# Sample recurrences with one eight-column product per state, and woven dense products taken column by column

## The chip, the core and the metric

The kernel runs on one core of one Trainium2 chip. The metric is the device time of one execution in microseconds; the profile beside it is of one execution. The engines are named as the profile names them: PE (matmul) and PEld (its weight load), DVE (vector), ACT (scalar), POOL and SP (here mostly issuers of transfers).

## The reference

One decoder layer for a prompt of 256 rows and 8 sample sequences of 4 rows, all with a model width of 2048 and with shared weights. Cut to what matters here:

```
h = x + 1/2 * SwiGLU_1(RMSNorm(x))
u = RMSNorm(h); P = u @ w_in
y_A = GatedDeltaNet(...)   # S_t = exp(g_t)(I - beta_t k_t k_t^T) S_{t-1} + beta_t k_t v_t^T ; o_t = S_t^T q_t
y_B = GLA(...)             # S_t = diag(exp(gk_t)) S_{t-1} + k_t v_t^T ;               o_t = S_t^T q_t
y_C = RWKV-7(...)          # S_t = S_{t-1} diag(w_t) + (S_{t-1} a_t) b_t^T + v_t k_t^T ; o_t = S_t r_t
m = sum_i sigmoid(P_gate_i) * (y_i @ w_branch[i]);  h = h + m @ w_out
x = h + 1/2 * SwiGLU_2(RMSNorm(h))
```

Each mixer has a chunked form. For a chunk, the incoming state S is multiplied twice: with the decayed keys, which gives the correction ("delta") z, and with the decayed queries, which gives the part of the output that comes from the old state. The sample group has 8 sequences of 4 tokens, and each is one chunk with a state of its own.

## The kernel before

**The dense products.** Activations stand transposed, 2048 as 16 tiles of 128 by 288 columns (256 prompt and 32 sample tokens). Each weight is split into a high and a low part and each activation too, so a 128x128 weight tile costs three matmuls of 288 columns (`three`, L336 to L338: `xh` by `hi`, `xl` by `hi`, `xh` by `lo`). Weights come in slots of 512 KB through a ring of four (`raw`, loaded by SP); ACT makes `hi` (L470), DVE makes `lo` (L607).

**The woven products.** The projections `inA`, `inB`, `inBt` and `gate` are not a phase of their own: they are cut into units and put between the steps of the three mixers, which run in the order C, A, B. `weave(n)` gives PE the next n units. Four slots are a group, which fills two PSUM banks, 6 and 7, one for each 128 output columns; a slot has four units `k`, and a unit is six matmuls:

```
if k == 0 and r == 0:
    pe.wait_ge(acc_empty, p["group0"] + it * p["groups"] + s // 4)
...
for c in range(2):
    mm = three(ps[:, 6 + c, 0:NT], q, (2 * k + c) * P, xh[:, 4 * r + k, :], ...
```

So a group is 16 units, 96 matmuls, and its two banks fill together. The other side is ACT's `weave`: after the last unit it copies both banks into `kept` (L533; L527 and L528 for `inA`), adds one to `acc_empty`, and sends `kept` to HBM. PE may begin the next group in the same two banks only then.

**The sample recurrences.** In the last block of each mixer (`n` = 32) PE goes through the states: six head pairs in C, six heads in A, three head pairs in B, each with 8 sequences (`s0C`, `s0A`, `s0B`, 128 x 8 x 128). For one of them in C and A the order is:

- For each of the 8 sequences PE makes two products with the state as weight and four columns moving: with `w` (L1191, L1674; it gives z) and with `rr` or the query (L1192, L1675; it gives the output). They go to banks 2 and 3, and `ss_z` is marked.
- ACT copies bank 3 into `ybuf` (L1306, L1742); DVE copies bank 2 into `zT` (L1461, L1864).
- PE transposes `zT` (L1196, L1679), DVE adds `zb` to it and spreads the result over the 8 sequences with the mask (`um`: L1465, L1867). In C it then spreads `vT` too (`vm`, L1466). `ss_z_kept` is marked.
- PE makes the output's products (L1200, L1201; L1681) and the state's update, 512 columns each: `bl` by `um` (L1205) and `kl` by `vm` (L1206) in C, `kd` by `um` (L1683) in A. `ss_os` is marked, and woven units follow (`sso` = 3 in C, `asso` = 2 in A).
- DVE scales the old state by its decay (L1469, L1871), adds the update (L1470, L1872) and adds the output's second part to `ybuf`.

In B there is no z. For each of two heads of a pair PE makes 8 products with half the rows of the state (L2010), then the rest (L2011, L2016); ACT copies the outputs.

What sets the order is this written order on each engine and its semaphores; no scheduler has a part in it. POOL loads and stores the states.

## Time and profile before

| | |
|---|---|
| time, median of 3 runs | 3584.94 us (3574.43 to 3591.28) |
| the profiled execution | 3578.71 us, of which 3576.5 us are its span |
| mean granted clock of TensorE, as a share of 2.4 GHz | 0.933 |
| PE busy | 3280.4 us, 92% of the span |
| DVE, ACT, POOL busy | 49%, 33%, 2% |
| the mixers with the woven products | 1080 to 2440 us of the span |
| their sample blocks | C from 1549 to 1752, A from 2164 to 2249, B from 2375 to 2414 us |

A row of the waits says which engine and line waited, for what, the sum, how often and the longest. A row of the timeline gives start, length, engine, line and tiles, and in brackets the idle time ahead of it with what ended it. A matmul in fp32 leaves two records in the trace, so 8 products are 16 of them. PE's matmuls are pipelined, so the step from one start to the next tells its pace, not the length of one.

### The profile page before, as it was taken

Reading aid. Unit: us, or ns where it says so; the run is one execution under the profiler, and the core shown is the slowest. Engines: PE = TensorE matmul, PEld = TensorE weight load, DVE = VectorE, ACT = ScalarE, POOL = GpSimd, SP = SyncE. Lnnn points to the kernel's source line nnn. Section 1 sums busy time; section 2 is a strip of 40 time slices with the busy share of each in tenths; the row PEclk is TensorE's granted clock in tenths of the full one; section 3 lists DMA queues with packets and bytes.
Section 4 is the critical chain, followed back from the end, with each engine's and each line's share of the span. In section 5 each row is a group of like instructions: output and inputs, shape, how many; then the busy total and the mean of one; then the engine's idle time right before and its main releaser. Section 6 shows DMA issues by size and latency. Waiting matters only on the chain.

```text
span 3576.5 us, 60087 instructions
## 1 busy us (share of the span) xinstructions
PE 3280.4 (92%) x23462; PEld 3132.4 (88%) x23462; DVE 1770.1 (49%) x2246; ACT 1175.4 (33%) x1511; POOL 69.0 (2%) x139
## 2 busy tenths in 40 slices
PE   7999999999799899888887898898999999999998
PEld 6999999999798788867687886788999999899997
DVE  4554345543446655544575543437644554445534
ACT  4333333332335322211243220316534333333332
POOL 2000000000000000000000000000000000000000
PEclk9999999999899999977798996769999999999999
DMA  4555455544454222222262233325644554455542
GB/s 134 164 164 165 155 149 164 165 156 137 119 164 142 88 82 88 72 78 78 81 188 87 75 92 86 111 81 167 202 141 141 164 164 155 156 159 164 165 147 91
DMA packets 596088, 472.52 MB, mean 132 GB/s; under 512 B 28871, under 2 KB 541279, under 8 KB 595597
## 3 DMA queue, kind: packets, MB, share of 16 engines
q1 hardware_dynamic: 578960, 435.53, 41.0%
q0 software_dynamic: 6288, 21.47, 2.1%
q10 hardware_dynamic: 10704, 13.61, 1.1%
q8 instruction: 98, 1.61, 0.2%
q14 instruction: 38, 0.31, 0.0%
HBM read 447.10 MB, written 23.38 MB: 132 GB/s over the span
## 4 chain that ended last, share of the span: by engine, by line
PE 82%; DVE 10%; ACT 4%; issue 2%; DMA 1%; POOL 0%; DVEq 0%; ACTq 0%; SPq 0%; POOLq 0%
PE ps L336 23%; PE ps L337 22%; PE ps L338 22%; DVE lo L607 2%; PE ps L939 1%; PE ps L929 1%; PE ps L461 1%; ACT hi L470 1%; PE ps L1205 1%; PE ps L1683 1%; PE ps L1206 1%; PE ps L1996 1%; DVE xl L777 0%; PE ps L934 0%; ACT kept L533 0%
## 5 line engine op out<-in xcount | busy, mean ns | idle before, releaser
L336 PE MATMUL ps<-xh,hi 128*128 128x288 f32 x4800 | 1473.1, 307 | 103.3 <-ACT kept L533 30.3
L337 PE MATMUL ps<-xl,hi 128*128 128x288 f32 x4800 | 1448.9, 302 | 0.0
L338 PE MATMUL ps<-xh,lo 128*128 128x288 f32 x4800 | 1448.0, 302 | 0.0
L607 DVE TENSOR_TENSOR lo<-raw,hi 128x1024 fp32r<-128x1024 f32 x820 | 981.6, 1223 | 610.6 <-ACT hi L470 601.7
L470 ACT ACTIVATE hi<-raw 128x1024 fp32r<-128x1024 f32 x820 | 839.1, 1053 | 858.6 <-PE ps L338 817.0
L336 PEld LDWEIGHTS ps<-xh,hi 128*128 128x128 f32 x4800 | 933.8, 195 | 146.4 <-issue 54.8
L337 PEld LDWEIGHTS ps<-xl,hi 128*128 128x128 f32 x4800 | 934.2, 195 | 0.7
L338 PEld LDWEIGHTS ps<-xh,lo 128*128 128x128 f32 x4800 | 932.9, 194 | 0.0
L336 PE MATMUL ps<-hidh,hi 128*128 128x288 f32 x1376 | 413.6, 301 | 26.5 <-DVE x L647 14.8
L337 PE MATMUL ps<-hidl,hi 128*128 128x288 f32 x1376 | 412.6, 300 | 0.0
L338 PE MATMUL ps<-hidh,lo 128*128 128x288 f32 x1376 | 410.0, 298 | 0.0
L336 PEld LDWEIGHTS ps<-hidh,hi 128*128 128x128 f32 x1376 | 263.9, 192 | 28.4 <-DVE x L647 15.7
L338 PEld LDWEIGHTS ps<-hidh,lo 128*128 128x128 f32 x1376 | 264.3, 192 | 0.0
L337 PEld LDWEIGHTS ps<-hidl,hi 128*128 128x128 f32 x1376 | 264.1, 192 | 0.0
L631 DVE TENSOR_TENSOR work<-ps,rstd 128x288 f32<-128x288 f32 x86 | 39.4, 458 | 334.4 <-PE ps L338 334.4
L491 ACT ACTIVATE work<-work 128x288 f32<-128x288 f32 x86 | 38.2, 444 | 485.0 <-DVE work L631 485.0
L336 PE MATMUL ps<-yh,hi 128*128 128x288 f32 x288 | 87.3, 303 | 13.9 <-ACT kept L533 7.0
L533 ACT ACTIVATE kept<-ps 128x576 f32<-128x576 f32 x33 | 21.5, 650 | 198.0 <-PE ps L338 192.6
L337 PE MATMUL ps<-yl,hi 128*128 128x288 f32 x288 | 86.5, 300 | 0.0
L338 PE MATMUL ps<-yh,lo 128*128 128x288 f32 x288 | 86.1, 299 | 0.0
L640 DVE TENSOR_TENSOR hidl<-prodt,hidh 128x288 f32 (+1 forms) x86 | 39.4, 459 | 62.1 <-ACT hidh L495 62.1
L336 PEld LDWEIGHTS ps<-yh,hi 128*128 128x128 f32 x288 | 55.5, 193 | 16.3 <-issue 8.5
(682 smaller groups left out, 2409.8 us busy)
## 6 DMA issues: line engine op xcount, KB each, us to landing
raw<-in_w_ff_up SPq DMA_DIRECT2D x688, 256.0 KB, 4.2
raw<-in_w_in SPq DMA_DIRECT2D x448, 256.0 KB, 3.0
raw<-in_w_ff_down SPq DMA_DIRECT2D x344, 256.0 KB, 3.2
raw<-in_w_out SPq DMA_DIRECT2D x64, 256.0 KB, 3.2
raw<-in_w_branch SPq DMA_DIRECT2D x48, 256.0 KB, 3.1
gatesD<-kept ACTq DMA_DIRECT2D x24, 288.0 KB, 3.1
gates<-gatesD SPq DMA_DIRECT2D x8, 864.0 KB, 7.2
raw<-in_w_branch SPq DMA_DIRECT2D x48, 128.0 KB, 3.4
```

The lines of the kernel that those rows point to most:

```text
L336: pe.matmul(out, w, rh, start=start, stop=False)
L337: pe.matmul(out, w, rl, start=False, stop=False)
L338: return pe.matmul(out, wl, rh, start=False, stop=stop)
L461: pe.matmul(ps[:, 7, 0:NT], ones[:, :], sq[:, k % 2, :], start=k == 0, stop=k == KD - 1).then_inc(sem("sq_used"), 1)
L470: act.activation(hi[:, q, :], raw[:, q, :], ACT.Copy).then_inc(hi_ready[q], 1)
L491: act.activation(work[:, 1, :], work[:, 0, :], ACT.Silu).then_inc(gate_ready, 1)
L607: dve.tensor_tensor(lo[:, q, :], raw[:, q, :], hi[:, q, :].bitcast(F32), SUB).then_inc(lo_ready[q], 1)
L631: dve.tensor_tensor(work[:, 0, :], ps[:, g % 2 * 2, 0:NT], rstd[:, :], MUL).then_inc(sem("gate_scaled"), 1)
L640: dve.tensor_tensor(hidl[:, bass.ds(m, 1), :], prodt[:, 1:2, :], hidh[:, bass.ds(m, 1), :].bitcast(F32), SUB).then_inc(hid_lo, 1)
L929: mm = pe.matmul(cell(0, q, n, n), t[at][0:n, q, :], t[a][0:n, q, :], start=True, stop=True)
L939: mm = pe.matmul(cell(2, q, n, n), t[a][0:n, q, :], t["tt"][0:n, q, :], start=True, stop=True)
L1205: pe.matmul(out, t["blT"][0:32, p, :], t["um"][:, four, :], start=True, stop=False)
```

## The change

It has three parts, and a renaming of semaphores with it.

- **Woven products, column by column.** A slot's four units are taken in another order: units 0 and 1 make all of its products for bank 6, units 2 and 3 those for bank 7. The bank 6 of a group is full two units before its end. ACT copies it then (`first_full`), and bank 7 after the last unit. PE starts a group when bank 6 was copied (`first_kept`), and waits for bank 7 (`acc_empty`) two units later.
- **One product of eight columns.** A tile `wr` (`rr2` in B) holds for each sequence the four columns of `w` beside the four of `rr`; in B the columns of the one head with zeros in the other's rows, beside those of the other head. So each state is loaded once. The results stand interleaved in one bank. DVE now makes both copies out of it; ACT's copy is gone.
- **Order around them.** In C `vm` is made ahead of the wait for `ss_z`, and PE makes `kl` by `vm` directly behind the eight products; only `bl` by `um` is left for later. In C, A and B the scaling of the old state is moved up behind the copies out of the eight products.

```diff
@@ pe weave @@
-                    if k == 0 and r == 0:
-                        pe.wait_ge(acc_empty, p["group0"] + it * p["groups"] + s // 4)
+                    G = p["group0"] + it * p["groups"] + s // 4
+                    n = G - PLAN["inA"]["group0"]
+                    c, half = divmod(k, 2)
+                    if k == 0 and r == 0:
+                        if n:
+                            pe.wait_ge(sem("first_kept"), n)
+                        else:
+                            pe.wait_ge(acc_empty, G)
+                    if k == 2 and r == 0:
+                        pe.wait_ge(acc_empty, G)
...
-                    for c in range(2):
-                        mm = three(ps[:, 6 + c, 0:NT], q, (2 * k + c) * P, xh[:, 4 * r + k, :],
-                                   xl[:, 4 * r + k, :], r == 0 and k == 0, r == 3 and k == 3)
+                    for kk in (2 * half, 2 * half + 1):
+                        mm = three(ps[:, 6 + c, 0:NT], q, (2 * kk + c) * P, xh[:, 4 * r + kk, :],
+                                   xl[:, 4 * r + kk, :], r == 0 and kk == 0, r == 3 and kk == 3)
+                    if k == 1 and r == 3:
+                        mm.then_inc(sem("first_full"), 1)
@@ act weave @@
-                    if k < 3 or s % 4 < 3:
+                    if k % 2 == 0 or s % 4 < 3:
                         continue
...
+                    c = k // 2
+                    if c == 0:
+                        act.wait_ge(sem("first_full"), n + 1)
...
+                    done = acc_empty if c else sem("first_kept")
...
-                        act.activation(kept[:, :, 0:NT], ps[:, 6:8, 0:NT], ACT.Copy).then_inc(acc_empty, 1)
+                        act.activation(kept[:, c, 0:NT], ps[:, 6 + c, 0:NT], ACT.Copy).then_inc(done, 1)
@@ pe, sample block of C (A alike, without the vm products) @@
                             for k in range(NSEQ):
-                                u = slice(TS * k, TS * k + TS)
-                                pe.matmul(ps[:, 2, u], t["s0"][:, k, :], t["w"][:, p, u], start=True, stop=True)
-                                mm = pe.matmul(ps[:, 3, u], t["s0"][:, k, :], t["rr"][:, p, u], start=True, stop=True)
+                                u = slice(2 * TS * k, 2 * TS * k + 2 * TS)
+                                mm = pe.matmul(ps[:, 2, u], t["s0"][:, k, :], t["wr"][:, p, u], start=True, stop=True)
                             e.mark(mm, "ss_z")
+                            e.need("ss_v_kept")
+                            for k in range(2):
+                                out = ps[:, k, :].rearrange("p (b v) -> p b v", v=P)
+                                pe.matmul(out, t["klT"][0:32, p, :], t["vm"][:, 4 * k:4 * k + 4, :], start=True, stop=False)
                             weave(U["ssz"])
...
-                                pe.matmul(out, t["blT"][0:32, p, :], t["um"][:, four, :], start=True, stop=False)
-                                mm = pe.matmul(out, t["klT"][0:32, p, :], t["vm"][:, four, :], start=False, stop=True)
+                                mm = pe.matmul(out, t["blT"][0:32, p, :], t["um"][:, four, :], start=False, stop=True)
@@ dve, sample block of A @@
                         e.need("ss_z")
-                        e.mark(dve.tensor_copy(t["zT"][:, :], ps[:, 2, 0:32]), "ss_zT_kept")
+                        e.mark(dve.tensor_copy(seqs(t["zT"][:, :]), pairs(ps[:, 2, 0:64])[:, :, 0, :]), "ss_zT_kept")
+                        e.link(dve.tensor_copy(seqs(ybuf[:, YA + h, t0:t0 + n]), pairs(ps[:, 2, 0:64])[:, :, 1, :]))
+                        s0 = t["s0", h % 2][:, :, :]
+                        e.link(dve.tensor_tensor(s0, s0, bc(t["pl"][:, h, :], 2, P), MUL))
                         e.need("ss_zt")
@@ pe, sample block of B @@
+                        for k in range(NSEQ):
+                            u = slice(2 * TS * k, 2 * TS * k + 2 * TS)
+                            mm = pe.matmul(ps[:, 0, u], s0[:, k, :], t["rr2"][:, p, u], start=True, stop=True)
+                        e.mark(mm, "B_ss_z")
                         for par in range(2):
-                            h, q = slice(64 * par, 64 * par + 64), 3 * par + p
-                            for k in range(NSEQ):
-                                u = slice(TS * k, TS * k + TS)
-                                pe.matmul(ps[:, par, u], s0[h, k, :], t["rr"][h, p, u], start=True, stop=True)
+                            q = 3 * par + p
@@ dve, features of B's sample block @@
-                e.link(dve.scalar_tensor_tensor(A("rr"), q_, 64 ** -0.5, A("rr"), MUL, MUL))
+                if n == P:
+                    e.link(dve.scalar_tensor_tensor(A("rr"), q_, 64 ** -0.5, A("rr"), MUL, MUL))
+                else:
+                    e.link(dve.memset(t["rr2"][:, :, :], 0.0))
+                    for par in range(2):
+                        h = slice(64 * par, 64 * par + 64)
+                        e.link(dve.scalar_tensor_tensor(pairs3(t["rr2"][h, :, :], par), ...
```

The renaming lets steps that come one after the other share a semaphore (`so_mt`, `so_sq`, `so_ex` become `solve_out`, and so on); the counts that are waited for go up in step.

What PE is given for one head pair of C's sample block, from the products with the state to the woven units behind the update, stood like this before (the first row is the first of eight such pairs of rows, and the three rows of a woven half unit stand once):

```order
L1191 MATMUL ps<-wCs,s0C 128x4
L1192 MATMUL ps<-rrCs,s0C 128x4
...
L336 MATMUL ps<-xh,hi 128x288
...
L1196 MATMUL ps<-ident,zTC 32x128
L1200 MATMUL ps<-qbCs,zCs 64x32
L1201 MATMUL ps<-qkCs,vTCs 64x32
...
L1205 MATMUL ps<-umC,blTCs 128x512
L1206 MATMUL ps<-vmC,klTCs 128x512
L1205 MATMUL ps<-umC,blTCs 128x512
L1206 MATMUL ps<-vmC,klTCs 128x512
```

and stands like this in the changed kernel:

```order
L1213 MATMUL ps<-wrC,s0C 128x8 x8
L1218 MATMUL ps<-vmC,klTCs 128x512 x2
L336 MATMUL ps<-xh,hi 128x288
...
L1221 MATMUL ps<-ident,zTC 32x128
L1225 MATMUL ps<-qbCs,zCs 64x32
L1226 MATMUL ps<-qkCs,vTCs 64x32
...
L1230 MATMUL ps<-umC,blTCs 128x512 x2
```

Sixteen products of four columns became eight of eight, and two of the four products of 512 columns moved from behind the wait for `um` to ahead of the transpose.

DVE's list for one head of A's sample block, from the copy of z to the last addition, before and then after:

```order
L1864 COPY zTA<-ps 128x32
L1866 TENSOR_TENSOR zAs<-ps,zbAs 32x128
L1867 TENSOR_TENSOR umA<-zAs,seqmask 32x1024
L1871 TENSOR_TENSOR s0A_223<-s0A_223,plAs 128x1024
L1872 TENSOR_TENSOR s0A_223<-ps,s0A_223 128x1024
L1875 TENSOR_TENSOR ybuf<-ps,ybuf 128x32
```

```order
L1906 COPY zTA<-ps 128x32
L1907 COPY ybuf<-ps 128x32
L1909 TENSOR_TENSOR s0A_222<-s0A_222,plAs 128x1024
L1911 TENSOR_TENSOR zAs<-ps,zbAs 32x128
L1912 TENSOR_TENSOR umA<-zAs,seqmask 32x1024
L1915 TENSOR_TENSOR s0A_222<-ps,s0A_222 128x1024
L1917 TENSOR_TENSOR ybuf<-ps,ybuf 128x32
```

The scaling of the state (L1871) moved from behind `um` to ahead of the addition that makes z (now L1909), and ACT's copy to `ybuf` joined DVE's list.

## Rows read from the trace of the kernel before

**Rows 1.** The page, its first part: busy time, share, instructions.

```profile
PE 3280.4 (92%) x23462; PEld 3132.4 (88%) x23462; DVE 1770.1 (49%) x2246; ACT 1175.4 (33%) x1511; POOL 69.0 (2%) x139
```

**Rows 2.** Busy time by stretch; the last three columns are clock, DMA share, GB/s.

```profile
1080.00:2440.00 1360.00, 1180.99 (x8153) 1062.97 (x8152) 711.66 (x983) 363.31 (x546) 48.20 (x71) 0.86 0.32 94
1549.00:1752.00 203.00, 176.37 (x1057) 137.88 (x1053) 82.64 (x115) 26.76 (x43) 15.77 (x23) 0.74 0.25 72
2164.00:2249.00 85.00, 72.55 (x321) 54.51 (x319) 29.61 (x39) 4.55 (x10) 8.12 (x10) 0.62 0.29 81
2375.00:2414.00 39.00, 38.21 (x187) 28.54 (x186) 16.98 (x19) 4.28 (x10) 2.68 (x3) 0.68 0.37 110
1826.00:1880.00 54.00, 51.63 (x383) 50.93 (x384) 50.33 (x80) 29.06 (x51) 0.00 (x0) 1.00 0.61 178
```

**Rows 3.** Who waited for the tile `kept`: total us, times.

```profile
  PE ps L336: 45.6, 32
```

**Rows 4.** Timeline, the border of two woven groups in A's convolution.

```profile
1852.49 0.29 PE L338 MATMUL ps<-xh,lo 128*128 128x288 f32 x1
1852.87 0.65 ACT L533 ACTIVATE kept<-ps 128x576 f32<-128x576 f32 x1 [0.82 <-PE ps L338]
1853.57 0.40 PE L336 MATMUL ps<-xh,hi 128*128 128x288 f32 x1 [0.79 <-ACT kept L533]
1853.81 0.29 PE L337 MATMUL ps<-xl,hi 128*128 128x288 f32 x1
1853.94 0.29 PE L338 MATMUL ps<-xh,lo 128*128 128x288 f32 x1
```

**Rows 5.** Timeline of PE: the four long waits for `kept`.

```profile
1451.47 0.61 PE L336 MATMUL ps<-xh,hi 128*128 128x288 f32 x1 [6.17 <-ACT kept L533]
1902.14 0.61 PE L336 MATMUL ps<-xh,hi 128*128 128x288 f32 x1 [5.04 <-ACT kept L533]
1939.10 0.61 PE L336 MATMUL ps<-xh,hi 128*128 128x288 f32 x1 [4.82 <-ACT kept L533]
2437.07 0.58 PE L336 MATMUL ps<-yh,hi 128*128 128x288 f32 x1 [7.03 <-ACT kept L533]
```

**Rows 6.** Timeline, one head pair of C's sample block.

```profile
1589.57 0.39 PE L1191 MATMUL ps<-wCs,s0C 128*128 128x4 f32 x2 [0.64 <-DVE s0C L1457]
1593.17 0.38 PE L336 MATMUL ps<-xh,hi 128*128 128x288 f32 x1
1594.95 1.21 DVE L1465 TENSOR_TENSOR umC<-zCs,seqmask 32x1024 f32<-32x1024 f32 x1
1596.20 1.21 DVE L1466 TENSOR_TENSOR vmC<-vTCs,seqmask 32x1024 f32<-32x1024 f32 x1
1597.47 0.43 PE L1200 MATMUL ps<-qbCs,zCs 32*64 32x32 f32 x4 [2.94 <-DVE vmC L1466]
1598.04 2.07 PE L1205 MATMUL ps<-umC,blTCs 32*128 32x512 f32 x2
1605.16 0.61 PE L336 MATMUL ps<-xh,hi 128*128 128x288 f32 x1
```

**Rows 7.** Timeline, one head of A's sample block.

```profile
2194.24 0.53 PEld L1675 LDWEIGHTS ps<-proj,s0A 128*128 128x128 f32 x2
2194.66 0.32 PEld L1674 LDWEIGHTS ps<-wAs,s0A 128*128 128x128 f32 x2
2198.09 0.19 DVE L1864 COPY zTA<-ps 128x32 f32<-128x32 f32 x1 [4.29 <-PE ps L1675]
2198.83 0.28 DVE L1866 TENSOR_TENSOR zAs<-ps,zbAs 32x128 f32<-32x128 f32 x1 [0.56 <-PE ps L1679]
2200.41 0.63 PE L1681 MATMUL ps<-dtAs,zAs 32*128 32x32 f32 x2 [1.69 <-DVE umA L1867]
2204.73 1.23 DVE L1871 TENSOR_TENSOR s0A<-s0A,plAs 128x1024 f32<-128x1024 f32 x1 [4.37 <-PE ps L1683]
```

**Rows 8.** Timeline, B's sample block, the products of one head.

```profile
2375.67 1.95 PE L2010 MATMUL ps<-rrBs,s0B 64*128 64x4 f32 x16
```

More of the change, by code:

```diff
@@ L930, in square @@
                 if turned:
-                    e.need("so_off_kept")
+                    e.need("solve_kept")
                 if second:
@@ L1091, in pe_mixC @@
             e.need("lora_act")
-            e.need("shift_rows")
+            e.need("rows_kept")
             for p in range(BT):
@@ L1240, in chunks, with seqs, pairs, pairs3 @@
             return ap.rearrange("p h (j t) -> p h j t", t=c)
+        def seqs(ap):
+            return ap.rearrange("p (b t) -> p b t", t=TS)
+        def pairs(ap):
+            return ap.rearrange("p (b w t) -> p b w t", w=2, t=TS)
+        def pairs3(ap, k):
+            return ap.rearrange("p h (b w t) -> p h b w t", w=2, t=TS)[:, :, :, k, :]
         def cums(cs, p0, b, tiles=3, long=CL):
@@ L1259, in act_mixC @@
                                       shB[:, k % 2, TP:TP + NSEQ * 7].rearrange("p (b t) -> p b t", t=7)[:, :, GAP:],
-                                      ACT.Copy), "compact")
+                                      ACT.Copy), "moved")
                 weave(U["shift"] // 20)
@@ L1303, in act_mixC @@
                         for p in range(3):
-                            weave(U["s0t"])
-                            e.need("ss_z")
-                            e.mark(act.activation(ybuf[:, YC + 3 * g + p, t0:t0 + n], ps[:, 3, 0:32], ACT.Copy), "ss_o_kept")
-                            weave(U["ssz"] + U["sso"] + U["s8t"])
+                            weave(U["s0t"] + U["ssz"] + U["sso"] + U["s8t"])
             weave(U["rec"] + U["fin"])
@@ L1332, in dve_mixC @@
                 if k > 1:
-                    e.need("compact")
+                    e.need("moved")
                 W = PW - GAP
@@ L1336, in dve_mixC @@
                 e.mark(dve.scalar_tensor_tensor(shB[:, k % 2, 0:W], shA[:, k % 2, 0:W], par1[:, R_MU + m:R_MU + m + 1],
-                                                proj[:, m, GAP:PW], MUL, ADD), "shifted")
+                                                proj[:, m, GAP:PW], MUL, ADD), "mixed")
                 weave(U["shift"] // 20)
-            e.need("compact", 2)
+            e.need("moved", 2)
             e.link(dve.memset(padC[:, :], 0.0))
@@ L1527, in maps_A @@
             al = Map(startA, y_a)
-            for k in ("w", "zb", "z"):
+            for k in ("w", "zb", "z") if n == P else ("zb", "z"):
                 t[k] = (al if n == P else m)(k + tag, [P, 6, P])
@@ L1709, in act_mixA @@
                                       cvA[:, m % 2, SEQW:PW].rearrange("p (b t) -> p b t", t=7)[:, :, 0:TS],
-                                      ACT.Silu), "A_silu")
+                                      ACT.Silu), "moved")
                 weave(U["conv"])
@@ L1740, in act_mixA @@
                     for h in range(6):
-                        e.need("ss_z")
-                        e.mark(act.activation(ybuf[:, YA + h, t0:t0 + n], ps[:, 3, 0:32], ACT.Copy), "ss_o_kept")
                         weave(U["assz"] + U["asso"])
             weave(U["afin"])
-            e.need("A_fin")
+            e.need("gate_free")
             e.link(act.activation(zgG[:, :, 0:TP], proj[:, 18:24, GAP:SEQW], ACT.Silu))
@@ L1755, in dve_mixA @@
             weave(U["hist"])
-            e.need("A_hist")
+            e.need("hist_turned")
             dve.wait_ge(sem("projA_landed"), 64)
@@ L1772, in dve_mixA @@
                 if m > 1:
-                    e.need("A_silu")
+                    e.need("moved")
                 cv = cvA[:, m % 2, 0:W]
@@ L1922, in maps_B @@
                 t["vm"] = m("vmB", [32, 2, NSEQ, P])
+                t["rr2"] = m("rr2B", [P, 3, 2 * 32])
             return t
@@ L2055, in act_mixB @@
                     for p in range(3):
-                        e.need("B_ss_os")
-                        for par in range(2):
-                            ins = act.activation(ybuf[:, YB + 2 * p + par, t0:t0 + n], ps[:, par, 0:32], ACT.Copy)
-                        e.mark(ins, "B_ss_o")
                         weave(U["bsso"])
             weave(U["bfin"])
-            e.need("B_fin")
+            e.need("gate_free")
             e.link(act.activation(proj[:, 12:18, 0:NT], proj[:, 12:18, 0:NT], ACT.Silu))
@@ L2087, in dve_mixB @@
             e.link(dve.memset(padB[:, :], 0.0))
-            e.need("b_notlead")
+            e.need("b_consts", 3)
             lead = (TP // CP) * (CP + 1)
@@ L2095, in dve_mixB @@
             e.link(dve.memset(tB[0]["s"][:, :, :], 0.0))
-            e.need("b_upper")
+            e.need("b_consts", 3)
             for b in range(3):
@@ L2142, in dve_mixB @@
                         weave(U["bsso"])
-                        e.need("B_ss_os")
+                        e.need("B_ss_z")
                         s0 = t["s0", p % 2][:, :, :]
                         e.link(dve.tensor_tensor(s0, s0, bc(t["pl"][:, p, :], 2, P), MUL))
+                        for par in range(2):
+                            e.link(dve.tensor_copy(seqs(ybuf[:, YB + 2 * p + par, t0:t0 + n]), pairs(ps[:, 0, 0:64])[:, :, par, :]))
+                        e.need("B_ss_os")
                         e.mark(dve.tensor_tensor(s0, psf[:, 2048:3072].rearrange("p (b v) -> p b v", v=P), s0, ADD), "s_new")
-                        e.need("B_ss_o")
                         for par in range(2):
```

210 lines of the change are left out of this document (113 added, 97 removed).

## The prediction

> **What bounds the kernel now.** I read the page first, for the engine that bounds. PE is busy for 92% of the span, DVE for half of it [rows 1]: what leaves PE's list, or a wait on it, is what can shorten the kernel. The change touches only the mixers, so I asked next for busy times by stretch. From 1080 to 2440 us PE is busy for 1181 of 1360 us at a mean clock of 0.86, that is, for part of the time at 1.2 instead of 2.4 GHz, and the sample blocks of C, A and B (203, 85 and 39 us) have 0.74, 0.62 and 0.68 [rows 2]. So there are two kinds of loss: waits, and low clock. Then I took each edit to its place in the timeline.
>
> **Borders of the woven groups.** The reader is to see how PE stands still between a group's last matmul and the next one's first: ACT starts its copy 0.38 us after the last matmul has started, needs 0.65 us, and PE goes on 1.08 us after its last start, where the pace behind it is 0.13 us (1853.81 to 1853.94) [rows 4]. A border costs 1.08 - 0.13 = 0.95 us. PE waited 32 times like this, 45.6 us by the profile [rows 3]. Four waits are long, 6.17, 5.04, 4.82 and 7.03 us [rows 5], 23.1 together; that leaves 22.5 us in 28 waits, 0.80 each, as in the row, where the profile counts 0.79 and the steps give 0.95.
>
> The change lets PE start in bank 6 when ACT has copied that bank, which it can do while PE fills bank 7 for two more units, 12 x 0.13 = 1.6 us. The trace has no copy of one bank alone; it lies between half of 0.65 us and the whole, and I take some 0.4 us. 0.38 + 0.65 is below 1.6, so bank 6 is free in time even by the upper bound. The same holds for bank 7, which PE needs 1.6 us into the next group. What hides ACT's work is thus two units of PE on either side. If ACT is late for another reason, PE waits as before; that is so at the four long waits, where ACT is held by work of the mixer ahead of its copy. They keep all but the difference of a full and a half copy, 0.65 - 0.4 = 0.25 us each, 1 us in all.
>
> Of the 28 x 0.95 = 26.6 us not all comes out. The units are woven between mixer steps, and where PE next needs a result of DVE, a border's 0.95 us was cover for it: PE gets there earlier and waits there. I estimate that for a third of the borders, in full or by half; no row shows it. And in A's convolution DVE is busy for 50.33 of 54 us [rows 2]. The 383 matmuls there are four groups of 96, so DVE's own work is 12.6 us a group against 96 x 0.134 = 12.9 us of PE's: the border comes out there, but little more would. I take three quarters: 20 us, and with the long ones **21 us** (bounds 12 and 27.6).
>
> **C, six head pairs.** Sixteen products take from 1589.57 to 1593.17, 3.60 us, 0.225 each [rows 6]. The trace has no product of eight columns. From below it costs as much as one of four, 0.225; from above as much as two, 0.45, and then nothing is saved. The step per product is far above what four moving columns can need when 288 of them pass in 0.13 us [rows 4], so it is the load of the state as weight that sets it, and that doesn't change. I take 0.225: 8 x 0.225 = 1.8 us saved.
>
> The wait for `um` and `vm` is 2.94 us, of which `vm` is 1.25 (1594.95 to 1596.20 is the step of one) [rows 6]. `vm` is now made while PE does one unit and the eight products, so 1.25 us go. The two products `kl` by `vm` are moved from behind that wait to ahead of the transpose. All four take from 1598.04 to 1605.16, 7.1 us [rows 6], at 1.2 GHz, since the woven matmul behind them lasts 0.61 us where the one behind the products with the state lasts 0.38. Two are 3.4 us there, and 1.7 us if they come while the clock is still at 2.4 GHz, as it is when the products with the state run. So moving them saves between nothing and 1.7 us; but if the clock falls before them, the unit behind them goes slow too: six matmuls of 0.13, which cost another 0.8 us.
>
> DVE has more to do behind `ss_z`: the copy to `ybuf` (0.2, as the copy of `zT`) and the scaling of the state (1.23) [rows 7]. They are hidden: PE has 1.7 to 3.4 us of products and one unit of 0.8 before its transpose, DVE needs 0.2 + 0.2 + 1.25. If that cover were gone it would cost what it costs in A, below.
>
> A head pair saves 1.8 + 1.25 = 3.05 us, less 0.8 or plus 1.7. I take 3.3, six times: **20 us** (bounds 14 and 28).
>
> **A, six heads.** The products save 8 x 0.225 = 1.8 us. But here no unit and no product stands between them and the transpose. DVE's path from the copy of `zT` to the addition was 2198.83 - 2198.09 = 0.74 us, and PE's transpose lies in it [rows 7]. Now it is 0.19 + 0.2 + 1.23 and three hand-overs of about 0.03, 1.7 us. So the addition, and everything behind it, comes 0.97 us later. Behind this DVE instruction are queued the addition and `um`, and PE waits for them with its update. What DVE no longer does behind the update is hidden by two woven units already. At an equal clock a head saves 1.8 - 0.97 = 0.83 us, 5 us in all. But the clock isn't equal. The second product of this head still takes 2194.66 - 2194.24 = 0.42 us [rows 7], twice the 0.225, so it runs at 1.2 GHz; the other 14 need 3.4 us up to the copy of `zT`, so the clock has come up as they begin, behind 12 dense matmuls. If the shorter step puts the eight under the low clock, they take 8 x 0.42 = 3.4 us, against 3.6 for 16 at full clock; then a head loses 0.97 - 0.2 = 0.8 us, 5 in all. I take the middle, **0 us** (bounds -5 and +5).
>
> The Trainium skill states, on the page TensorE: Matmul & The Clock Gate, in the section What's actually happening, that the throttled clock is the default and activity releases it. By that rule an edit that takes activity out of a stretch and adds a wait to it, as in A, gets a lower clock for it; A would then give -5 instead of 0, and the sum below would be 42 instead of 47. The trace agrees as far as it goes: A's block, with the least matmul work in it, has the lowest clock of the three.
>
> **B, three head pairs.** Two times 8 products of half the rows take 1.95 us each at full clock [rows 8]; 8 with all rows take 8 x 0.225 = 1.8. That is 2.1 us saved, 6.3 in all. The zeros of `rr2` and one more short instruction of DVE stand ahead of the features for which PE waits, at some 0.25 us each (between 0.19 and 0.28, the short ones of [rows 7]): 0.5 us, once. The rest of DVE's new work lies under four woven units. **6 us** (bounds 3 and 8). ACT's copies are gone from a list that is idle there. The renamed semaphores are waited for at the same points; nothing for them.
>
> **Sum.** 21 + 20 + 0 + 6 = 47 us against the profiled execution's 3578.7: 3532 us. The median of the runs shown, 3584.9, lies 6 us above it. I take the middle of 3532 and 3584.9 - 47 = 3538: **3535 us**. By the bounds: 27.6 + 28 + 5 + 8 = 69 saved, and 12 + 14 - 5 + 3 = 24; so 3513 to 3558, and 3 us wider on either side for the scatter of the three runs.
>
> **Rivals.** First: the eight-column products save nothing, since they cost as two, or as the time gained is lost to the low clock. For it speaks the clock in all three sample blocks [rows 2]; against it, that in C the wait for `vm` goes at any clock. Then 21 + 6 x 1.25 = 28 us are left: 3553. Second: the waits at the borders come back in full elsewhere, on DVE's `lo` or on the mixers' results. For it speaks DVE's 93% in the convolution [rows 2], against it that ordinary borders stand in long runs of woven units. Then 20 + 6 = 26 us: 3555. Third: everything comes out at its upper bound, and the time at the clock's low level shrinks with it: below 3510. Fourth, on the other side: the clock. C's, A's and B's sample blocks are at 2.4 GHz for 48, 24 and 36% of the time (0.74 is (1 + 0.48) / 2), 97 + 20 + 14 = 131 us. If the thinned-out steps no longer bring the clock up, that work takes twice the time, +131 us. It outweighs the 47 us when 36% of these stretches fall low, and is slower by over 0.5% from half of them: 3584.9 + 65 - 47 = 3603. The rule of the Trainium skill's page TensorE: Matmul & The Clock Gate named above is the one that speaks for it. Against it: the dense units that bring the clock up are all still there.
>
> **Chances.** My forecast, 3513 to 3558 with both kinds of gain: 0.65. The first rival 0.12, the second 0.1, the third 0.08, the fourth 0.05. The first two end inside the range or at its edge; the range 3510 to 3560 leaves out the third and the fourth and a little of the scatter. 0.5% of the time, 18 us, is about what a measurement of this kernel can tell from no change: faster from 3567 down. All but the fourth and a piece of the first two lie there: faster 0.9, same 0.07, slower 0.03.
>
> **What would show it.** After the change, PE's waits on `kept` should be about four long ones, some 22 us, with no ordinary ones left. Eight products should take 1.8 us at full clock. In C, PE's wait ahead of L1225 (L1200 now) should be some 1.7 us; in A the wait ahead of the update should be longer by 0.97 us, 2.7 instead of 1.7 [rows 7]. PE's waits on `lo` in the woven part should grow by less than 5 us. I would be wrong if the clock in the three sample blocks changed by more than 0.05, or if PE waited for bank 6 at ordinary borders.

## The result

The changed kernel takes 3532.16 us (median of 4 runs, 3511.55 to 3537.79) where the kernel before took 3583.88 on the same chip (median of 4, 3574.43 to 3591.28): a ratio of 0.985, 95% interval 0.982 to 0.988, or 52 us less. The profiled execution took 3535.43 us, of which 3533.5 are its span, 43 us less than the span of before; TensorE's mean granted clock is 0.932 (before 0.933). The ratios here and below leave out one run of the kernel before that took 6248 us, in the second of the three sets below.

The page of the changed kernel, its first part, answers to [rows 1]:

```profile
PE 3250.3 (92%) x23222; PEld 3107.7 (88%) x23222; DVE 1773.5 (50%) x2266; ACT 1179.1 (33%) x1550; POOL 68.8 (2%) x139
```

PE has 240 matmul records fewer: of 96 products with the state in C, 96 in A and 48 in B there are half as many now, and each has two records. PE's waits in the changed kernel, 1080 to 2400 us (who waited for whom, total us, times, longest):

```profile
PE ps L336 <- ACT kept L548: 25.5, 6, 9.9
PE ps L336 <- DVE lo L628: 16.7, 5, 5.8
PE ps L1718 <- DVE umA L1912: 16.0, 6, 2.8
PE ps L1225 <- DVE umC L1505: 10.1, 6, 1.7
```

The 45.6 us in 32 waits for `kept` [rows 3] are 25.5 us in 6: the ordinary borders are gone. The four long ones stand (6.01, 4.81, 4.25 and 9.87 us), with two short ones below half a us. PE's waits on `lo`, by which the second rival would have shown itself, are 16.7 us and were 16.1. Half a group's copy costs 0.41 us, as estimated; for `inA` it is still two copies, 0.39 and 0.20 us. The row of the tile `kept` (minimum, median and maximum in ns) and of PE's waits for it:

```profile
L548 ACT ACTIVATE kept<-ps x66: 390/411/415, 1373.5 to 2394.2; 128x288 f32<-128x288 f32 x66
  PE ps L336: 25.9, 7
```

The longest wait stands at the end of B. It was 7.03 us [rows 5] and is 9.87 now. ACT's timeline and the first dense matmul behind the mixers show why:

```profile
2376.02 1.06 ACT L481 ACTIVATE hi<-raw 128x1024 fp32r<-128x1024 f32 x1 [2.13 <-PE ps L338]
2380.76 0.41 ACT L548 ACTIVATE kept<-ps 128x288 f32<-128x288 f32 x1 [3.68 <-PE ps L338]
2381.19 1.28 ACT L2099 ACT_TABLE_LOAD   x1
2382.48 1.65 ACT L2099 ACTIVATE proj<-proj 128x1728 f32<-128x1728 f32 x1
...
2394.21 0.41 ACT L548 ACTIVATE kept<-ps 128x288 f32<-128x288 f32 x1
```

```profile
2395.09 0.58 PE L336 MATMUL ps<-yh,hi 128*128 128x288 f32 x1 [9.87 <-ACT kept L548]
```

ACT now copies twice per group, so it has a wait in the middle of a slot that it did not have. Here that wait, 3.68 us for the last group's first column, stands ahead of B's last features (L2099 and what follows), and these stand ahead of the second copy.

PE's side of one head pair in C answers to [rows 6] (all at 1.2 GHz but the eight products, which are at 2.4):

```profile
1578.48 1.99 PE L1213 MATMUL ps<-wrC,s0C 128*128 128x8 f32 x16 [0.63 <-DVE s0C L1494]
1580.40 3.77 PE L1218 MATMUL ps<-vmC,klTCs 32*128 32x512 f32 x4
1585.71 0.42 PE L1221 MATMUL ps<-ident,zTC 128*32 128x128 f32 x1
1587.82 0.43 PE L1225 MATMUL ps<-qbCs,zCs 32*64 32x32 f32 x4 [1.69 <-DVE umC L1505]
1588.39 3.78 PE L1230 MATMUL ps<-umC,blTCs 32*128 32x512 f32 x4
```

PE steps on from the eight products after 1580.40 - 1578.48 = 1.92 us: one of eight columns costs 0.24 (in B 0.22, 2353.84 - 2352.07 us over eight, below), and one of four cost 0.225. The wait for `um` is 1.69 instead of 2.94. The moved pair `kl` by `vm` costs 3.8 us, as it did.

One head of A answers to [rows 7]:

```profile
2161.30 3.41 PE L1712 MATMUL ps<-wrA,s0A 128*128 128x8 f32 x16
2164.82 0.19 DVE L1906 COPY zTA<-ps 128x32 f32<-128x32 f32 x1 [5.01 <-PE ps L1712]
2165.05 0.19 DVE L1907 COPY ybuf<-ps 128x32 f32<-128x32 f32 x1
2165.27 1.23 DVE L1909 TENSOR_TENSOR s0A<-s0A,plAs 128x1024 f32<-128x1024 f32 x1
2166.53 0.28 DVE L1911 TENSOR_TENSOR zAs<-ps,zbAs 32x128 f32<-32x128 f32 x1
2166.85 1.21 DVE L1912 TENSOR_TENSOR umA<-zAs,seqmask 32x1024 f32<-32x1024 f32 x1
2168.11 0.63 PE L1718 MATMUL ps<-dtAs,zAs 32*128 32x32 f32 x2 [2.65 <-DVE umA L1912]
2168.56 3.76 PE L1720 MATMUL ps<-umA,kdAs 32*128 32x512 f32 x4
```

The reader is to see two things: the eight products take 3.41 us, 0.43 each, at 1.2 GHz, nearly twice the price in C (so do those of five of the six heads; the first head's run at 2.4 GHz); and the scaling of the state stands between the two copies and the addition, so that the wait for `um` is 2.65 instead of 1.69 us.

B's middle pair, in the timeline of PE: first before, then after.

```profile
2390.03 1.95 PE L2010 MATMUL ps<-rrBs,s0B 64*128 64x4 f32 x16
2391.90 0.40 PE L2011 MATMUL ps<-qkBs,vTBs 32*128 32x32 f32 x2
2392.24 3.21 PE L2010 MATMUL ps<-rrBs,s0B 64*128 64x4 f32 x16
2395.37 0.63 PE L2011 MATMUL ps<-qkBs,vTBs 32*128 32x32 f32 x2
2395.93 3.68 PE L2016 MATMUL ps<-vmB,klTBs 32*64 32x512 f32 x8
2399.55 0.61 PE L336 MATMUL ps<-xh,hi 128*128 128x288 f32 x1
```

```profile
2352.07 1.85 PE L2047 MATMUL ps<-rr2B,s0B 128*128 128x8 f32 x16
2353.84 0.63 PE L2051 MATMUL ps<-qkBs,vTBs 32*128 32x32 f32 x4
2354.40 3.06 PE L2056 MATMUL ps<-vmB,klTBs 32*64 32x512 f32 x8
2357.39 0.61 PE L336 MATMUL ps<-xh,hi 128*128 128x288 f32 x1
```

The products of this pair's second head ran at the low clock before, 3.21 us and not 1.95; in the first pair the second head took 2.56 us, and in the third 1.95. The pair takes 2357.39 - 2352.07 = 5.32 us instead of 2399.55 - 2390.03 = 9.52.

By stretch, each cut at a matmul that all kernels have (for C's sample block from the first transposition of a state to the last one), with the time at 1.2 GHz in brackets (us). The kernels of the last two columns have one part of the change each:

| stretch | before | changed | woven columns alone | recurrences alone |
|---|---|---|---|---|
| ahead of the mixers | 1076.6 | 1076.6 | 1074.1 | 1075.1 |
| C, prompt | 484.7 (34) | 477.6 (41) | 477.6 (41) | 484.6 (34) |
| C, samples | 179.8 (106) | 162.7 (99) | 176.4 (99) | 156.0 (82) |
| C's end to A | 64.9 | 66.0 | 65.7 | 66.5 |
| A, prompt | 361.2 (68) | 352.2 (64) | 351.4 (61) | 354.4 (51) |
| A, samples | 88.8 (62) | 89.3 (79) | 91.3 (68) | 86.8 (68) |
| A's end and B's prompt | 119.7 (68) | 118.8 (61) | 119.7 (68) | 118.0 (61) |
| B, samples | 50.5 (27) | 38.3 (17) | 49.5 (27) | 40.8 (20) |
| B's end | 10.9 | 13.7 | 13.7 | 11.2 |
| behind | 1139.4 | 1138.4 | 1137.5 | 1138.5 |

A stretch of one trace is not exact where the clock moves. The changed kernel and five of the kernels below have the same code up to the end of C's sample block, and it reads 151.5 (75), 154.7 (82), 159.5 (92), 159.6 (92), 162.7 (99) and 162.7 (99) there. A's sample block, which three of the kernels below share with the changed one, reads 86.6 (72), 86.7 (72), 89.3 (79) and 89.3 (79). Each us at the low clock costs about half a us, and how long it stays low differs between executions. So a term of a few us needs the medians of many runs, or a step that repeats.

### The profile page after: what moved, and what is told of

It reads as the page before. It is cut to its first block, busy times and chain, and to the rows that moved or that the text cites. A ratio compares the mean times of both kernels' runs of the same rounds, so it can differ in the third digit from the quotient of the medians.

```text
span 3533.5 us, 59711 instructions
## 1 busy us (share of the span) xinstructions
PE 3250.3 (92%) x23222; PEld 3107.7 (88%) x23222; DVE 1773.5 (50%) x2266; ACT 1179.1 (33%) x1550; POOL 68.8 (2%) x139
## 4 chain that ended last, share of the span: by engine, by line
PE 80%; DVE 13%; ACT 4%; issue 2%; DMA 1%; POOL 0%; DVEq 0%; ACTq 0%; SPq 0%; POOLq 0%
PE ps L336 22%; PE ps L337 22%; PE ps L338 22%; DVE lo L628 2%; PE ps L961 1%; PE ps L951 1%; PE ps L472 1%; ACT hi L481 1%; PE ps L1230 1%; PE ps L1720 1%; PE ps L1218 1%; PE ps L2035 1%; PE ps L1712 1%; DVE cvA L1813 1%; DVE xl L798 0%
## 5 line engine op out<-in xcount | busy, mean ns | idle before, releaser
L548 ACT ACTIVATE kept<-ps 128x288 f32<-128x288 f32 x66 | 26.2, 409 | 292.4 <-PE ps L338 292.0
L336 PE MATMUL ps<-yh,hi 128*128 128x288 f32 x288 | 86.9, 302 | 16.7 <-ACT kept L548 9.9
L336 PEld LDWEIGHTS ps<-yh,hi 128*128 128x128 f32 x288 | 55.1, 191 | 18.9 <-ACT kept L548 10.1
```

What stands on the lines that cost most here:

```text
L336: pe.matmul(out, w, rh, start=start, stop=False)
```

## The experiments

Ten kernels ran, each beside the kernel before on its chip. The kernel before had medians of 3581.65, 3583.08 and 3581.41 us in the three sets (12, 9 and 9 runs).

### The woven columns alone

The kernel before, with the first part of the diff alone (`first_full`, `first_kept`, the order of the units) and the shared semaphores of the triangular solve.

> The kernel before with the first part of the change alone: woven products column by column, accumulators copied one by one (and the semaphores of the triangular solve shared, as in the changed kernel, since two new ones are needed). By the prediction's term it saves 21 us (12 to 27.6). By the rival theory read from the changed kernel's trace, that borders give back more than assumed because the next wait on DVE takes it, it saves some 13 us. If the borders came out in full it would be 27. The waits on the copy shrink to the four long ones under either.

Measured: 3569.14 us (3558.90 to 3578.18), ratio 0.9967 (0.9951 to 0.9982), 12 us less (6 to 18). Its own trace is of its shortest run and shows 20 us, of which 4.4 lie ahead of and behind the mixers, where the two kernels are the same; that leaves 15. The step is thus 12 us by the medians and 15 in the one trace, and the forecast's 21 lies outside the interval. The waits for `kept` are 25.4 us in 6, so the change does what was said of it; the rest went elsewhere, in pieces that the trace shows:

- C's prompt stage, some 5 us: its 13 ordinary borders are 12.4 us by the prediction's price, and the stage is 7.1 us shorter. It has 41 us at 1.2 GHz where it had 34, which is some 3.5 us, and PE waits 6.0 us for `qbCp` where it waited 4.1: borders just ahead of a result of DVE. With the same work the clock falls at places where it had not. These are its windows from 1250 to 1285 us (length, busy PE, PEld, DVE, ACT and POOL, clock, DMA share, GB/s), of before and of this kernel:

```profile
1250.00:1285.00 35.00, 31.61 (x289) 29.49 (x291) 18.55 (x31) 7.61 (x16) 0.00 (x0) 1.00 0.24 70
```

```profile
1250.00:1285.00 35.00, 33.48 (x276) 31.06 (x276) 19.05 (x31) 8.49 (x18) 0.00 (x0) 0.85 0.22 65
```

 Of a lead of 7.95 us at 1255 us (of the kernel before) 3.27 are left at 1352 us, behind four such falls; part of it comes back later, where the kernel before has falls that this one has not. What PE did before the first fall was short products of the chunk's recurrence (64 to 128 columns), as in the kernel before at the same place. The first two falls stand at the same place in nine of the ten kernels here that have the woven columns, and in neither of the two that have not; the tenth, with the lighter convolution, has the same code up to there and none of the four. What decides it is open.
- C's end to A, where three borders gave nothing: 65.7 us instead of 64.9. PE's wait there for a transfer (`smA`) is 3.7 us where it was 1.9. That transfer is issued behind DVE's last work of C and lands 13.6 us later, which a border does not shorten.
- A's sample block, where no border stands: 2.5 us longer, with 6 us more at the low clock.
- B's end, 2.8 us: 13.7 instead of 10.9, the wait of ACT shown above.
- A's convolution, 0.32 us a group: DVE becomes the bound (below).

### The recurrences alone

The changed kernel, with the woven part as before.

> The changed kernel with the woven products as before (both columns in turn, one copy of both banks at the end of a group): the sample recurrences alone. By the prediction's terms for C, A and B it saves 26 us against the kernel before. If the two parts add up, what it saves and what the columns alone save sum to the 51 us of the whole. If the gain of the borders comes partly from the recurrences' clock, they don't.

Measured: 3540.12 us (3533.78 to 3545.95), ratio 0.9888 (0.9873 to 0.9903), 41.5 us less (36 to 46). The forecast had 26 for C, A and B together, so this one is off as well, on the other side. 12.5 + 41.5 = 54 is the 52 of the whole within the intervals (some 5 us on either side of each part): the parts add up. Of the 44 us that its trace, of its shortest run, shows, 23.8 are in C's sample block, 2.0 in A's, 9.7 in B's, and 6.8 in A's prompt stage, where this kernel has the same instructions as the kernel before and 17 us less at the low clock. Those 6.8 us are a difference of clock between two executions or one that the earlier blocks bring with them; that wasn't told apart.

### A: the scaling behind `um`

```diff
@@ dve, sample block of A @@
-                        s0 = t["s0", h % 2][:, :, :]
-                        e.link(dve.tensor_tensor(s0, s0, bc(t["pl"][:, h, :], 2, P), MUL))
                         e.need("ss_zt")
...
+                        s0 = t["s0", h % 2][:, :, :]
+                        e.link(dve.tensor_tensor(s0, s0, bc(t["pl"][:, h, :], 2, P), MUL))
```

> The changed kernel, but in A's sample block DVE scales the old state behind um instead of ahead of the addition that makes z. By the theory that this order costs 0.97 us per head, PE's wait for um falls from 2.65 to 1.7 us and the step from one head to the next from 13.95 to 13.0 us while the clock stays low, 5 us in all; if the shorter step brings the clock of this block back from 1.2 GHz, it is up to 1.5 us more for a head, 14 us in all. By the rival theory that the clock alone sets the step, it stays near 13.7 us and the time the same.

Measured: 3521.40 us (3511.30 to 3532.14), ratio 0.9831 (0.9812 to 0.9850). PE's wait for `um` is back to what it was:

```profile
PE ps L1718 <- DVE umA L1910: 10.1, 6, 1.7
```

A head's step is 13.0 us in three of five, where it was 13.99 in four of five. So the early scaling costs 0.96 us a head at this clock, 6 in the block, as worked out in the prediction, and nothing pays for it. The block is 7 us shorter than in the changed kernel (82.3, 72 at the low clock). The median is 11 us less, but the runs of the two kernels overlap, and this kernel's trace has a C block of 151.5 us with unchanged code; the step shows the 6 us, the time does not.

### A: one woven unit between the products and the transpose

`assz` is 1 instead of 0 and `asso` 1 instead of 2: the unit covers the scaling.

> The changed kernel, but of the two woven units behind each head's update in A one is moved between the eight products and the transpose, where PE waits for DVE. At the low clock a unit is 1.44 us, of which PE's wait for zT (0.4) and DVE's longer list (0.97) are covered: the step falls from 13.95 to some 12.8 us, 7 us in all. By the theory that the clock decides, the dense units stand apart now and the block stays at 1.2 GHz, which it does already in the profiled execution of the changed kernel; but executions in which it came up would lose it, and the gain would be under 7 us.

Measured: 3524.20 us (3521.57 to 3529.51), ratio 0.9843 (0.9830 to 0.9856). A head's step is 12.9 us in four of five, and A's sample block 82.5 us where it was 89.3. With cover the early scaling is harmless; the same was had by making it late (82.3 us). The unit also covers PE's wait for `zT`, which was not told apart.

### C: `kl` by `vm` late again

Both products back behind the wait for `um`, in pairs with `bl` by `um`, as before; `vm` is still made early.

> The changed kernel, but in C's sample block PE makes the products kl by vm behind the wait for um again, as before; vm is still made early. By the prediction's step, having them ahead of the transpose saves between nothing and 1.7 us a pair, or costs 0.8 where the clock falls before them. In the changed kernel's trace they run at the low clock (3.77 us for both), so this theory expects no change or a gain of up to 0.8 us a pair, 5 us in all. The rival theory says they cover DVE's scaling of the state: without them PE waits for um 2.6 instead of 1.7 us, and the block is 5 us slower.

Measured: 3530.70 us (3528.11 to 3537.61), ratio 0.9851 (0.9836 to 0.9867), against 3532.16: no difference. The wait is 2.4 us at the longest instead of 1.7, as the products no longer cover it, and C's sample block is 159.1 (89). Moving them early is worth nothing that these runs can tell: C's block lies within the readings of the same code above (151.5 to 162.7), and the pair runs at 1.2 GHz in either place.

### A: sixteen products of four columns

```diff
@@ pe, sample block of A @@
-                            u = slice(2 * TS * k, 2 * TS * k + 2 * TS)
-                            mm = pe.matmul(ps[:, 2, u], s0[:, k, :], t["wr"][:, h, u], start=True, stop=True)
+                            for u in (slice(2 * TS * k, 2 * TS * k + TS), slice(2 * TS * k + TS, 2 * TS * k + 2 * TS)):
+                                mm = pe.matmul(ps[:, 2, u], s0[:, k, :], t["wr"][:, h, u], start=True, stop=True)
```

> The changed kernel, but A's sample block makes 16 products of four columns per head out of the same tile instead of eight of eight. It shows the price of one product at either clock, with all else equal. If the load of the state sets the price, eight products less are worth 1.8 us at full clock and 3.4 us at the low one, so with the low clock that A has now the step from head to head grows from 13.99 to 17.4 us. If the columns set it, it stays at 13.99. If the clock comes up again with the longer step, as in the kernel before, the step is at some 14.5 us and the time of the whole grows by 3 us only.

Measured: 3542.28 us (3539.49 to 3550.34), ratio 0.9892 (0.9876 to 0.9908), 10 us more than the changed kernel, 13.3 in A's sample block (102.6 instead of 89.3). The first rival, that the product of eight columns saves nothing, falls: it saves 2.2 us a head on average. Two heads of this kernel show where the clock stands:

```profile
2144.59 6.82 PE L1712 MATMUL ps<-wrA,s0A 128*128 128x4 f32 x32
2161.99 4.06 PE L1712 MATMUL ps<-wrA,s0A 128*128 128x4 f32 x32
```

In three of the six heads sixteen take 6.82 us, 0.43 each, which is the price at 1.2 GHz. Two of the steps that begin with such a head are 17.40 us, and 17.40 - 13.99 = 3.41 us is what eight products less are worth with all else, the clock too, equal. In the other three heads sixteen take 3.6 to 4.1 us, some 0.25 each and nearly the price at 2.4 GHz. The first of them has the clock up in both kernels, and its step is 14.14 us for 12.36, 1.8 us more. For the third and fourth the clock is up with sixteen alone, and their steps are 14.61 and 14.34 us for 13.99: there most of what the shorter list gives is taken by the clock.

### A's convolution with one tap less

```diff
@@ dve, convolution of A @@
-                for j in (1, 2):
+                for j in (1,):
```

It leaves out one of the four taps of the convolution.

> The changed kernel with one tap of the convolution of A left out (DVE makes two multiply-adds per channel instead of three, 0.55 us less of 3.3 us; the conv, its outputs and what follows from them are other numbers). In the changed kernel's trace a woven group takes 13.2 us there, 96 matmuls at 0.134 need 12.86, and DVE's list has no gap. If DVE bounds this stretch, the groups take 12.86 us without the tap and six of them give 2 us. If not, they stay at 13.2 us.

Measured: 3524.77 us (3522.15 to 3527.26), ratio 0.9835 (0.9820 to 0.9851). A group's step in the convolution was 13.8 us in the kernel before, is 13.17 in the changed one and 12.80 here, which is 96 matmuls of 0.133. Over six groups that is 2 us; the rest of the 7 us less is not explained by the convolution (this trace has 10 us less at the low clock in C's prompt stage, where the code is the same). DVE's list in the changed kernel has no gap:

```profile
1805.93 1.22 DVE L628 TENSOR_TENSOR lo<-raw,hi 128x1024 fp32r<-128x1024 f32 x1
1807.08 0.38 DVE L1811 TENSOR_SCALAR cvA<-proj,par 128x312 f32<-128x312 f32 x1
1807.49 1.12 DVE L1813 SCALAR_TENSOR_TENSOR cvA<-proj,par,cvA 128x312 f32<-128x312 f32 x2
1808.65 0.54 DVE L1814 SCALAR_TENSOR_TENSOR cvA<-proj,par,cvA 128x312 f32<-128x312 f32 x1
1809.23 1.22 DVE L628 TENSOR_TENSOR lo<-raw,hi 128x1024 fp32r<-128x1024 f32 x1
```

1809.23 - 1805.93 = 3.30 us a slot, 13.2 a group, which is the step. A border gives 0.63 us there and not 0.95, before DVE holds PE up.

### C and A: a unit under `um`

The late scaling in A, and in C and A one woven unit taken from behind the update and put between the transpose and the wait for `um` (`sso` 2 and `asso` 1).

```diff
@@ pe, sample blocks of C and A @@
                             e.mark(pe.transpose(ps[0:32, 4, 0:P], t["zT"][:, :], ident[:, :]), "ss_zt")
+                            weave(U["szt"])
                             e.need("ss_z_kept")
```

> The changed kernel with the late scaling in A, and in A's and C's sample blocks one woven unit moved from behind the update to between the transpose of z and the wait for um. PE waits 1.7 us there per head and pair. By the theory that this wait is a plain gap, a unit fills 1.44 us of it at the low clock and 0.8 at the full one: 5 to 8 us less in each block beside the kernel with the late scaling alone, some 12 in all. By the theory that the clock decides, parting the dense units keeps the clock low: A stays at 1.2 GHz throughout and C loses some of its time at 2.4 GHz, and the gain is under 5 us.

Measured: 3499.74 us (3496.99 to 3507.07), ratio 0.9772 (0.9758 to 0.9786), 83 us less than the kernel before and 32 less than the changed one. The waits for `um` are all but gone (two rows of the waits, 1540 to 2250 us: PE L1226 and L1720 with 1.7 us each in 6), the block of C is 141.1 us (61 at the low clock, 99 in the changed kernel; below all six readings of the unchanged block, as are the 139.0 us of the second kernel of the next section), that of A 76.3 (68). The changed kernel's waits for `um`, 16.0 + 10.1 = 26.1 us, became 3.4. In C the low clock went with the waits; in A the late scaling alone had 72 us at it already. One head of A in this kernel:

```profile
2160.43 0.40 PE L1717 MATMUL ps<-ident,zTA 128*32 128x128 f32 x1 [0.35 <-DVE zTA L1908]
2160.48 0.59 PE L336 MATMUL ps<-xh,hi 128*128 128x288 f32 x1
...
2162.52 0.63 PE L1720 MATMUL ps<-dtAs,zAs 32*128 32x32 f32 x2 [0.25 <-DVE umA L1912]
```

### The last group of B

`bgk`, the woven units ahead of B's last features, is 10 instead of 12, in the changed kernel and in the kernel of the section above.

> The changed kernel with this one number alone (two woven units fewer ahead of B's last features). My theory: the stretch from B's sample block to the branch products falls from 13.7 to about 11 us, ACT's wait of 3.68 us for the first column of the last group is gone, and the time is 2 to 3 us below the changed kernel's: about 3529.5 where that took 3532.2. Rival, it is the clock or the two units are paid behind: 3532, the stretch at 13.7 or the stretch shorter and the one behind it longer.

> The fastest version so far (in C's and A's sample blocks one woven unit between the transpose and the wait for um, in A the scaling of the state behind um) with one number more changed: two woven units fewer stand ahead of B's last features, so that the first column of the last woven group fills behind ACT's Silu, Ln and Exp and not ahead of them. My theory: in the changed kernel ACT waits 3.68 us in the middle of a slot for that column, its features of B's last block come later, and the stretch from B's sample block to the branch products is 13.7 us instead of the 10.9 of before. Then it goes back to about 11 us, and the kernel takes 2 to 3 us less than its fellow: about 3497.5 us where that one took 3499.7. Rival: those 2.8 us come from something else (the low clock of that stretch, 6 us of it instead of 3); then the stretch stays at 13.7 and the time within 1 us of 3499.7. A second rival: the two units come behind and are paid there, so that the stretch is shorter and the time the same.

Measured: 3528.57 us (3511.48 to 3530.95), ratio 0.9843 (0.9820 to 0.9866), in the changed kernel, and 3503.67 us (3490.91 to 3505.51), ratio 0.9768 (0.9748 to 0.9788), in the other. In both B's end takes 11.5 us instead of 13.7, and the long wait is shorter, here in the changed kernel with 10:

```profile
2383.03 0.58 PE L336 MATMUL ps<-yh,hi 128*128 128x288 f32 x1 [6.07 <-ACT kept L548]
```

ACT goes from its last split (2367.76) straight to the features (2368.84). So the mid-slot wait of ACT is the cause of 2.2 of the 2.8 us. Of the kernel's time nothing certain is left: 3.6 us less in one pair, 3.9 more in the other, and B's sample block is 1.6 and 4.7 us longer, with 3 and 10 us more at the low clock. The rival that it is paid elsewhere is not excluded.

## Why the prediction was right, and where only in sum

3535 us was forecast and 3532.16 measured. The sum is right because two wrong terms have opposite signs, and that is luck: the woven columns alone gave 12 us and not 21, the recurrences alone 41.5 and not 26. The range, built from the bounds of the terms, held; the third rival (below 3510 us) and the fourth did not come.

**Borders, 21 us forecast, 12 measured (6 to 18; 15 in the trace).** The mechanism is as forecast: the ordinary waits for `kept` are gone, and half a copy costs 0.41 us. What failed is "I take three quarters". The discount for borders that were cover was made for waits on DVE alone. The clock took some 3.5 us in C's prompt stage, where the prediction looked for it in the sample blocks only, and the three borders ahead of A gave nothing. And "they keep all but the difference of a full and a half copy" holds for three of the long waits (they are 0.2, 0.2 and 0.6 us shorter) and is wrong for the fourth: it grew from 7.03 to 9.87 us, since a second copy per group is a second place where ACT waits in order. DVE's bound in the convolution was seen, but its work was put at the 12.6 us a group for which it is busy, where its list takes 13.2 from start to start, with some 0.03 us between instructions, so the border gives 0.63 and not 0.95.

**C, 20 us forecast.** Measured 18 to 24: the block of before in the one trace, 179.8, against the mean of the six readings, 158.5, is 21 us, of which the columns alone have 3.4; with the recurrences alone it is 23.8. The products (0.24 each, for 0.225) and `vm` (1.25 off the wait, 1.69 left) came as worked out. "Or plus 1.7" for the early `kl` by `vm` is not there: both pairs run at the low clock, and put back late they cost nothing that these runs can tell.

**A, 0 us forecast, -0.5 in the trace,** and +2 in two others with the same block. Both halves of the reasoning hold. The wait grew by 0.96 us (forecast 0.97), and the eight products take 3.41 us (forecast 3.4 at the low clock); the block's time at 1.2 GHz rose from 62 to 79 us (to 72 in those two). A head's step went from 13.6 to 14.0, between the middle and the lower bound. That the products are worth 2.2 us a head nevertheless, and 3.4 at an equal low clock, is shown by the kernel with sixteen.

**B, 6 us forecast, 10 to 12 measured.** The step that failed is "two times 8 products of half the rows take 1.95 us each at full clock": the row was that of the first head of the first pair. The second heads took 2.56, 3.21 and 1.95 us, since the clock fell on the way in the first two pairs. So 4.51, 5.16 and 3.90 became 1.85 each, 8.0 us for the 6.3 of the forecast. The updates gained too: three times 3.68 us became 1.94, 3.06 and 3.44, 2.6 us, as the block had 27 us at the low clock and has 17. One row was too few; the second head and the next pair were in the same view.

**Rivals.** The first (eight columns save nothing) is excluded in A. The second (borders come back elsewhere in full) is excluded by the 12 us of the columns alone (6 to 18), though nearly half of it is true. The fourth (the clock turns the sign) did not come, but its mechanism is at work in A and in C's prompt stage. I named a change of the clock by more than 0.05 in a sample block as a sign against me; in A it fell by more: 0.56 in the stretch below, where [rows 2] has 0.62. In B it rose by more, and over C's whole block it hardly moved (by the table 0.71 and 0.70, in A 0.65 and 0.56, in B 0.73 and 0.78). So that sign came true and the time was met all the same: it was no test of the sum.

The windows of the changed kernel for A's and B's block (columns as in [rows 2], PE, PEld, DVE, ACT, POOL first):

```profile
2140.00:2230.00 90.00, 74.86 (x275) 57.02 (x276) 33.93 (x45) 8.61 (x14) 8.88 (x10) 0.56 0.32 91
2343.00:2396.00 53.00, 43.13 (x240) 35.68 (x239) 32.55 (x44) 19.73 (x28) 3.56 (x4) 0.78 0.31 94
```

The Trainium skill's page TensorE: Matmul & The Clock Gate, named in the prediction (section What's actually happening), says that activity releases the clock. The traces agree in part: in A's block 70 and 74% of the time is at 1.2 GHz with sixteen products (62 of 88.8 us before, 68 of 91.3 with the woven columns alone) and 78 to 88% with eight in five kernels. But with sixteen products and the early scaling it is 83%, so the number of products alone does not tell it.

## What to carry to other kernels

A wait on a copy out of a full bank can be had back by filling the banks one after the other, but every extra copy is a new point of order on the copying engine: look what stands behind it in that list before it is put there, and count only what the next engine (here DVE, 13.2 us a group against PE's 12.8) leaves. An early instruction is free only under cover: the same scaling of 1.23 us costs nothing in C and 0.96 us a head in A. And where a chain of short steps ends in a wait, dense work put into that wait can be worth as much as the waits or more: with one unit in each of 12 steps the kernel takes 22 us less than with the late scaling alone (3499.7 against 3521.4), where the waits for `um` had some 20. In C the block is 17 us below the mean of the six readings, and the waits there had 10; in A it is 6 us below the late scaling alone, and the waits had 10. C has 38 us less at the low clock than in the changed kernel, and 14 less than the lowest of the six.

## What was unexpected in the hardware

- The clock falls, and stays low, in stretches in which PE is hardly idle. In C's prompt stage it fell behind short products, and the window has PE busy for 33.48 of 35 us, where the kernel before had 31.61 and a clock of 1.00; part of the higher share is the low clock's own doing, as the same products take longer. In C's sample block PE is busy for 15.3 of the 17 us from 1580.3 to 1597.3 us, two pairs of updates of 32 rows (3.77 us each) among them, and all of it is at 1.2 GHz.
- Fewer products can take nearly as long: in one head of A eight took 3.41 us and sixteen 4.06; in three others sixteen took 6.82.
- The same code reads 151.5 to 162.7 us in one block, by 75 to 99 us at the low clock, in profiles of six kernels that differ only behind it.
